# One of two lanes of attention probabilities transposed by VectorE in 32x32 blocks instead of by TensorE and a copy

## What is computed

```python
def _dilated_attention(q, k, v, rel_bias):
    for g, (offs, bias, kg_all, vg_all) in enumerate(cfg):
        s = jnp.einsum('bqhd,bqkhd->bhqk', qb[:, :, g], kg.astype(jnp.float32))
        s = s + bias[None, :, None, :]
        s = jnp.where(valid[None, None], s, NEG_INF)
        lse = jax.nn.logsumexp(s, axis=-1)
        p = jnp.exp(s - lse[..., None])
        outs.append(jnp.einsum('bhqk,bqkhd->bqhd', p, vg.astype(jnp.float32)))
        lses.append(lse)
    wts = jax.nn.softmax(jnp.stack(lses, axis=0), axis=0)
    out = jnp.sum(wts * jnp.stack(outs, axis=0), axis=0)
```

## Time and profile before

| what | value |
|---|---|
| median of three runs | 1304.11 us |
| lowest, highest | 1302.74, 1304.68 us |
| the profiled execution, its own time | 1302.51 us |
| its span in the trace | 1300.7 us |
| PE busy | 1283.2 us, 99% of the span |
| DVE busy | 929.7 us, 71% |
| ACT busy | 679.3 us, 52% |

### The profile page before, as it was taken

How to read it: one execution, slowest core, us unless ns; L and a number is a source line. 1 busy time by engine, 2 the same in 40 slices (tenths; PEclk the granted TensorE clock), 3 DMA queues, 4 the chain that set the end, 5 groups by cost and what they waited for, 6 DMA issues and landing times.

```text
span 1300.7 us, 16758 instructions
## 1 busy us (share of the span) xinstructions
PE 1283.2 (99%) x6242; PEld 1057.4 (81%) x6242; DVE 929.7 (71%) x1298; ACT 679.3 (52%) x976; POOL 125.9 (10%) x190
## 2 busy tenths in 40 slices
PE   9999999999999999999999999999999999999997
PEld 6888888888888888888887777888888887788886
DVE  6878948986678956677875677667895656655674
ACT  7444537755444546544445567644444735566542
POOL 1000003711000000000001230000000133200000
PEclk9999999999999999999999999999999999999999
DMA  9665645228565655666564643466564496445541
GB/s 311 216 201 189 210 140 203 66 82 263 191 194 194 202 186 162 195 194 194 194 196 158 231 162 119 149 194 194 194 226 154 170 293 215 156 137 179 174 149 33
DMA packets 149505, 236.29 MB, mean 182 GB/s; under 512 B 10080, under 2 KB 104464, under 8 KB 148928
## 3 DMA queue, kind: packets, MB, share of 16 engines
q1 hardware_dynamic: 144432, 222.26, 52.6%
q0 software_dynamic: 4640, 12.81, 3.3%
q10 hardware_dynamic: 368, 0.37, 0.1%
HBM read 233.27 MB, written 4.47 MB: 183 GB/s over the span
## 4 chain that ended last, share of the span: by engine, by line
PE 91%; DVE 4%; ACT 3%; issue 1%; POOL 0%; DMA 0%; POOLq 0%; SPq 0%; ACTq 0%; DVEq 0%
PE acc L628 20%; PE acc L630 20%; PE acc L629 20%; PE acc L661 7%; PE acc L662 7%; PE acc L665 7%; PE misc L704 4%; DVE wl L2086 1%; ACT wh L1538 1%; PE misc L1339 1%; PE misc L888 1%; PE misc L1195 1%; ACT xh L1584 0%; PE acc L868 0%; ACT hn L1570 0%
## 5 line engine op out<-in xcount | busy, mean ns | idle before, releaser
L2086 DVE TENSOR_TENSOR wl<-raw,wh 128x2048 fp32r<-128x2048 f32 x199 | 450.6, 2270 | 183.5 <-ACT wh L1538 182.8
L1538 ACT ACTIVATE wh<-raw 128x2048 fp32r<-128x2048 f32 x205 | 383.5, 1894 | 125.3 <-PE acc L665 104.2
L628 PE MATMUL acc<-wh,xh 128*128 128x512 f32 (+1 forms) x832 | 324.5, 390 | 3.3 <-DVE xl L2132 1.6
L630 PE MATMUL acc<-wh,xl 128*128 128x512 f32 (+1 forms) x832 | 322.5, 388 | 0.0
L629 PE MATMUL acc<-wl,xh 128*128 128x512 f32 (+1 forms) x832 | 322.3, 387 | 0.0
L628 PEld LDWEIGHTS acc<-wh,xh 128*128 128x128 f32 x832 | 156.2, 188 | 36.7 <-DVE wl L2074 1.8
L630 PEld LDWEIGHTS acc<-wh,xl 128*128 128x128 f32 x832 | 156.2, 188 | 32.2
L629 PEld LDWEIGHTS acc<-wl,xh 128*128 128x128 f32 x832 | 156.2, 188 | 31.1
L1633 ACT ACTIVATE sg<-acc,rstd 128x256 f32<-128x256 f32 x88 | 41.4, 475 | 240.4 <-PE acc L630 240.3
L2252 DVE STREAM_TRANSPOSE aT<-a_n 32x384 f32<-32x384 f32 (+1 forms) x256 | 137.1, 536 | 3.9
L661 PE MATMUL acc<-wh,ah 128*128 128x512 f32 x320 | 124.8, 390 | 0.0
(11 more groups left out here) (365 smaller groups left out, 1613.1 us busy)
## 6 DMA issues: line engine op xcount, KB each, us to landing
raw<-in_ffn_w_in_dram SPq DMA_DIRECT2D x170, 512.0 KB, 4.8
raw<-in_ffn_w_out_dram SPq DMA_DIRECT2D x88, 512.0 KB, 4.3
raw<-in_w_in_dram SPq DMA_DIRECT2D x64, 512.0 KB, 4.7
raw<-in_fox_w_in_dram SPq DMA_DIRECT2D x24, 512.0 KB, 4.2
raw<-in_ple_w_gate_dram SPq DMA_DIRECT2D x16, 512.0 KB, 4.4
raw<-in_mla_w_o_dram SPq DMA_DIRECT2D x8, 512.0 KB, 4.0
raw<-in_fox_w_o_dram SPq DMA_DIRECT2D x8, 512.0 KB, 4.4
raw<-in_w_out_dram SPq DMA_DIRECT2D x8, 512.0 KB, 4.4
```

The source lines that it names most:

```text
L628: pe.matmul(dst, hi, rhs_h, start=first, stop=False)
L630: return pe.matmul(dst, lo, rhs_h, start=False, stop=last)
L1538: act.activation(wh[:, s, 0:n], raw[:, s, 0:n], ACT.Copy).then_inc(hi_done, 1)
L2086: dve.tensor_tensor(wl[:, s, 0:n], raw[:, s, 0:n], wh[:, s, 0:n].bitcast(F32), ALU.subtract)\
```

## The change

Lane 0's probabilities are no longer transposed by PE. In `even(i)`, PE transposes lane 1 alone. DVE no longer copies bank 2; in that place it waits for lane 0's exponentials and issues 16 block transposes from `pr2` to `pT2`. Each takes 32 partitions and four 32x32 blocks, 128 elements per partition, and writes them to another quarter of the partitions where needed. A new semaphore, `p_turned`, tells PE in `odd(i)` that lane 0 is ready. PE waits for it ahead of PV, in place of the read of bank 2. Bank 2 now takes the PV result alone, so its counters change. DVE's first score sum of `odd(i)`, which writes `pr2` lane 0, waits for `p_turned` too.

```diff
@@ PE, even(i) @@
                 if i:
                     j = i - 1
-                    for lane in range(2):
-                        pe.wait_ge(exp_done, 2 * j + lane + 1)
-                        open_m(2 + lane, hr[2 + lane] + (2 - lane) * j)
-                        for m in range(4):
-                            mm = turn(2 + lane, slice(m * P, m * P + P), pr2[:, lane, m * P:m * P + P])
-                        mm.then_inc(m_ready[2 + lane], 1)
+                    pe.wait_ge(exp_done, 2 * j + 2)
+                    open_m(3, hr[3] + j)
+                    for m in range(4):
+                        mm = turn(3, slice(m * P, m * P + P), pr2[:, 1, m * P:m * P + P])
+                    mm.then_inc(m_ready[3], 1)
@@ PE, odd(i) @@
-                    pe.wait_ge(m_read[2], hr[2] + 2 * j + 1)
+                    pe.wait_ge(p_turned, j + 1)
                     pe.wait_ge(m_read[3], hr[3] + j + 1)
+                    open_m(2, hr[2] + j)
@@ DVE, even(i) @@
                 if i:
-                    dve.wait_ge(m_ready[2], hf[2] + 2 * i - 1)
-                    dve.tensor_copy(pT2[:, 0, :], M[:, 2, :]).then_inc(m_read[2], 1)
+                    dve.wait_ge(exp_done, 2 * i - 1)
+                    for m in range(16):
+                        a, o = m % 4, m // 4
+                        src = pr2[QUAD * a:QUAD * a + QUAD, 0, :].rearrange("p (m o r) -> p m o r", m=4, o=4)
+                        dst = pT2[QUAD * o:QUAD * o + QUAD, 0, :].rearrange("p (m a r) -> p m a r", m=4, a=4)
+                        e = dve.transpose(dst[:, :, a, :], src[:, :, o, :])
+                    e.then_inc(p_turned, 1)
@@ DVE, odd(i) @@
                             dve.wait_ge(win_in[i % 2], WIN_IN[i])
+                            if i:
+                                dve.wait_ge(p_turned, i)
```

More of the change, by code:

```diff
@@ L68 @@
 NU = len(UNITS)
-U_FILLS = (2 * NU, 2 * NU, 2 * NU, NU)
+U_FILLS = (2 * NU, 2 * NU, NU, NU)
 U_FIRST = 6
@@ L378, in build @@
         fox_exp = sem("fox_exp")
+        p_turned = sem("p_turned")
         lane_ready = [sem(f"lane_ready{i}") for i in range(2)]
@@ L2751, in odd @@
                     grp, n = UNITS[i - 1]
-                    dve.wait_ge(m_ready[2], hf[2] + 2 * i)
+                    dve.wait_ge(m_ready[2], hf[2] + i)
                     w = 1 if grp == 0 else 2
@@ L2774, in combine @@
                 dve.wait_ge(exp_done, 2 * NU)
-                dve.wait_ge(m_read[2], hr[2] + 2 * NU)
+                dve.wait_ge(m_read[2], hr[2] + NU)
                 link(dve.tensor_tensor(low, nm[:, :, 0, :], nm[:, :, 1, :], ALU.min))
@@ L3056, in _ @@
                 .then_inc(bg_in, 16)
-            pool.wait_ge(m_ready[2], HEADS["b2"][0][2] + 2 * NU)
+            pool.wait_ge(m_ready[2], HEADS["b2"][0][2] + NU)
             pool.dma_start(fg[:, :], bass.AP(I["final_gain_2"].tensor, 0, [[0, P], [1, D]])).then_inc(fg_in, 16)
```

## The result

The changed kernel takes 1319.0 us (median of four runs, 1316.8 to 1321.1), against 1304.2 us before. The ratio is 1.0118, with a 95% interval from 1.0106 to 1.0130: slower by 14.8 us, and inside the stated range. The profiled execution took 1316.76 us, 14.25 us more than the profiled one of before; its span is 1314.9 us.

What follows compares the result with a forecast made beforehand. PE bounds the kernel before; after the change a DVE-ACT loop decides, moving the last PV from 1195.48 to 1207.24 us, +11.8 us with PE's 3.5 us saving swallowed: 1304.1 + 11.8 = 1315.9 us, range 1308 to 1322.

Steps and rivals of the forecast that it cites:

- PE's saving: On PE's path, four transposes of 0.109 us removed in each of eight units: 3.5 us saved.
- DVE's idle time has the wrong place: DVE's 43.2 us idle exceeds 34.0 us added work, but most lies between odd(i)'s maxima and the next even split.
- loop: DVE, ACT and DVE in sequence: seven periods of 15.3 to 17.5 us, longer than PE's 14.1 and 14.6 us.
- A: From start of score sums to next even step's split: maxima, ACT's exponentials, copy and `wh`; 5.70 to 7.63 us.
- B: Even step's split and copy of k on DVE: 2.54 us for two heads, 2.81 for four, 2.21 for even(8).
- E(8): End of the transposes in even(8), when PE may start the last PV; predicted at 1207.24 us.
- row of four: Trace's four block transposes of 256 elements per partition, read as 1.78 us, 0.445 us each, to estimate the new pitch.
- PE's waits: PE waiting ahead of PV for DVE's transposes: eight waits, 1 to 3 us each, 15 us in sum.
- The cover holds: Rival: DVE's 43.2 us idle time takes the 34.0 us, PE never waits, gain 3.5 us, 1300.6 us; chance 0.08.
- p: Pitch of one 128-element block transpose on DVE, estimated at 0.303 us, bounded by 0.221 and 0.445 us.
- E(7): End of the transposes in even(7), predicted at 1190.37 us; PE's work behind it reaches 1206.45 us.
- Rivals 2 and 3: Transposes overlap, pitch 0.221 us, 1305.4 us, chance 0.06; small transposes floor near 0.445 us, 1334 us, 0.08 with anything slower.

Runs made afterwards that it cites:

- plain copy: Against the changed kernel, one plain copy of lane 0 from pr2 to pT2 replaces each unit's sixteen transposes, leaving lane 0 untransposed; 1301.2 us, ratio 0.9981.
- moved version: Against the changed kernel, the same sixteen transposes moved from DVE's even step to the end of the odd step before; 1299.1 us, ratio 0.9965.
- early `wh`: Against the changed kernel, only ACT's list differs: its odd step splits weight groups w+2 and w+3 ahead of the exponentials; 1300.6 us, ratio 0.9976.
- twelve transposes: Against the changed kernel, twelve block transposes per unit instead of sixteen (unit 0 keeps sixteen), last quarter of lane 0's keys stale; 1308.4 us, ratio 1.0034.

## Why the prediction was right

**PE's saving** of 3.5 us: right, 3.48 us by the plain copy.

**DVE's idle time has the wrong place**: right. The same work in the same kernel costs 14.2 us in one place of DVE's list and nothing in another.

**The loop's terms.** A is 6.84, 5.70, 6.84, 7.62, 6.47, 7.62 and 7.42 us in the profile after, in sum 48.51 us where the prediction had 48.73. B is the same. The transposes are the term that was mis-sized: 5.07 us for sixteen and not 4.85. E(8) is at 1208.87, predicted 1207.24; the difference of 1.63 us is 8 x 0.22 = 1.76 for the transposes, less 0.22 for A, and 0.09 for a later start. What the prediction had wrong is the pitch of the row of four, from which it subtracted. It took 1.78 us for four of 256 elements from the first such row of that feed-forward; the three behind it are longer:

```profile
953.45 1.78 DVE L2252 STREAM_TRANSPOSE aT<-a_n 32x256 f32<-32x256 f32 x4
955.25 0.69 DVE L2259 TENSOR_TENSOR al<-aT,ah 128x512 fp32r<-128x512 f32 x1
...
958.17 1.79 DVE L2252 STREAM_TRANSPOSE aT<-a_n 32x256 f32<-32x256 f32 x4
959.98 0.69 DVE L2259 TENSOR_TENSOR al<-aT,ah 128x512 fp32r<-128x512 f32 x1
...
962.90 1.79 DVE L2252 STREAM_TRANSPOSE aT<-a_n 32x256 f32<-32x256 f32 x4
964.73 0.69 DVE L2259 TENSOR_TENSOR al<-aT,ah 128x512 fp32r<-128x512 f32 x1
```

These take 1.80, 1.81 and 1.83 us, so the four rows have a mean of 0.451 us each and not 0.445. Less the 0.135 us to the row of six, that gives 0.316 us, against 0.317 measured. An error of 0.006 us in one row was counted twice in each of 128 transposes. The mean durations, without the gaps between the transposes, lie on one line:

```profile
L2252 DVE STREAM_TRANSPOSE aT<-a_n 32x384 f32<-32x384 f32 x192 | 109.3, 569 | 2.8
...
L2252 DVE STREAM_TRANSPOSE aT<-a_n 32x256 f32<-32x256 f32 x64 | 27.9, 436 | 1.0
```

569 less 436 is 133 ns for 128 elements, so 303 ns for the new size, which is what it took. That the predicted pitch was also 0.303 us is chance: here the pitch is 0.317 us, the duration and a gap of 0.014 us.

**The last unit.** The prediction had PE arrive 0.8 us ahead of E(8), at full clock. It arrived 0.86 us behind it, because of the slow clock behind the wait of 3.06 us. With 1.63 us for E(8) this makes 2.5 us, the distance between the predicted 11.8 us and the 14.25 us of the profiled runs. That the granted clock "stays there", at 1.00, was the wrong sentence: it was read from a stretch in which PE never waited. The remaining 0.6 us of the 14.8 us between the medians lie within the scatter of the runs.

**PE's waits.** Eight were predicted, 15 us in sum; six came, 12.3 us. In the third unit and the last PE was slowed by the clock and so came no earlier than DVE. This did not move the end in the third unit, where the loop decides; it did in the last.

**The rivals.** "The cover holds" is what the plain copy, the moved version and the early `wh` show, with the gain of 3.5 us that it named. Here it did not hold. The prediction let it hold for p below 0.21 us, but there its sum is zero and the gain is not yet made: for the whole gain E(7) has to fall from 1190.37 to 1175.9 us (1195.48 - 3.48 - 16.08), which takes a p of 0.17 us. Rivals 2 and 3 are out by the measured 0.317 us: the transposes do not overlap, and a small one is cheaper than the smallest seen before. The Trainium skill's 311 ns for a 128x128, in "VectorE: DVE Perf Modes", section "The three transpose paths", stands there for bf16 and for 32x32 blocks that stay where they are. It does not apply here: for the whole transpose of fp32, four pieces took sixteen instructions at 0.317 us. The Trainium skill's rule in "VectorE: DVE Perf Modes", section "The TRN2 errata", that SBUF operands pay a fixed latency per instruction, agrees with the trace: 0.30 us for 128 elements, of which 0.17 us do not depend on their number. The estimate of 0.291 us from its formula, which is for `tensor_tensor`, is 4% below the 0.303 us measured.

## What to carry to other kernels

An engine's idle time is worth something only at the place where it lies. Before moving work onto an engine with enough idle time in sum, write down for one period what stands between two of its fixed points, with the other engines' parts in it, and compare that with the period of the engine that bounds. If it is longer, look for the wait inside the loop and put the new work into that wait: here one block of DVE's list, moved by half a unit, turned +14.8 us into -4.8 us against before (3.5 us of it in the units, the rest within the scatter).

## What the runs showed of the hardware

- Block transposes of 32x128 fp32 from SBUF to SBUF take 303 ns each, 317 ns from start to start. They do not overlap each other; DVE's copies and splits overlap their successor by 0.08 us (2.29 us long, 2.21 us from start to start), but a score sum does not overlap the maximum that reads it (1093.08 + 0.68 against a start at 1093.80).
- A PE that had been busy without a break and then waited for 1.8 to 3.1 us could come back at a lower granted clock. In the changed kernel's first profile it was 0.66, 0.75 and 0.63 in the 3 to 5 us behind the waits of 2.51, 2.20 and 3.06 us; in its second, 0.66, 0.68 and 0.69 behind waits of 2.46, 3.05 and 3.07 us, but 1.00 behind one of 2.12 us; with twelve transposes 0.63 behind a wait of 1.79 us, but 1.00 behind one of 1.78 us. With 0.9 us of matmuls ahead of each wait it was 1.00 behind waits of up to 1.95 us. Sixteen pooling matmuls took 5.1 to 5.4 us behind such a wait in place of 3.65 us. What decides in the cases between is left open.
